# Up products of a gated FFN: three products of 256 columns, or one of 512 and one of 256 with the halves added by VectorE

## The chip, the cores and the metric

The kernel runs on one core of a Trainium2 chip (trn2). Times are device microseconds (us) of one execution. A core has TensorE (PE in the rows: MATMUL, with the weight loads under PEld), VectorE (DVE), ScalarE (ACT), GpSimd (POOL) and SyncE (SP), each with a stream of its own; they meet only at semaphores. TensorE writes its results to PSUM, eight banks of 512 f32 columns in each of 128 partitions.

## What is computed

A model of four layers over 256 tokens of width 1024. The first two layers end in this FFN; their mixers, and the two mixture-of-experts layers behind them, are not touched by the change.

```
DFF = 2816                                  # D_FF
def conv_glu_ffn(n, w_up, conv_w, conv_b, w_down):      # n: (1, 256, 1024)
    s = n.shape[1]
    gate, up = jnp.split(n @ w_up, 2, axis=-1)          # w_up: (1024, 2 * 2816)
    gp = jnp.pad(gate, ((0, 0), (CONV_WIDTH - 1, 0), (0, 0)))
    conv = conv_b
    for j in range(CONV_WIDTH):                         # 3 taps along the tokens
        conv = conv + gp[:, j:j + s] * conv_w[j]
    return (jax.nn.silu(conv) * up) @ w_down
```

## The kernel before

**Numbers.** Every large product is made of fp32r operands that are split in two: `w_high` is the weight rounded to fp32r, `w_low` the rest, and the same for x and the hidden values. `product` (L1327 to L1331) adds high by high, high by low and low by high into one PSUM region, three MATMULs with a weight load ahead of each. ScalarE writes `w_high` from the loaded `raw` chunk (L460, two halves of 1024 columns), VectorE writes `w_low` as raw minus w_high (L788, two halves). In the FFN the weights are the stationary operand and x the moving one, so the products come out turned: 128 hidden channels by 256 tokens.

**Chunks and the ring.** The weights come as chunks of 128 x 2048 f32 (1 MB) into a ring of three slots. A chunk's `raw` slot is loaded again when `w_low` of it is written, and its `w_high` and `w_low` slots are written again when TensorE has counted `chunk_used` for it. ScalarE and VectorE split a chunk two ahead (`AHEAD`) of the one in use.

**One FFN** (`glu`, once in each engine's stream) is 22 tiles of 128 channels, in 11 pairs. TensorE's order is: up, up (tiles 0 and 1); ten times a turn of up, up, down (`turn`); one last down. An up (`up`, L1511) takes one chunk: eight k steps for the gate half and eight for the up half, each step one `product`. Gate goes to columns 0 to 255 of bank 4 + u, up to columns 256 to 511 of the same bank, u being the tile's place in its pair. A down (`down`) takes one chunk and adds a pair's share to banks 0 to 3: eight products of 512 columns. The down of a turn belongs to the pair before, so a pair's hidden values have one more turn to be ready in; only the last down has no turn in between: its pair's ups stand in the last turn, with just that turn's down between them and it.

**A tile's elementwise work** (buffers `conv` and `gate` are halves of rope_a, `hid` a half of rope_b, under which names they stand in the rows):

```
ACT  wait chunk_used -> conv = Identity(bank, scale w2, bias b)   L553, then split of a chunk (u = 0)
DVE  conv[1:] += bank * w1 (L940); conv[2:] += bank * w0 (L943)
ACT  gate = Silu(conv)                                            L558
DVE  hid = gate * up half of the bank                             L946
ACT  gh = high part of hid                                        L564
DVE  gl = hid - gh                                                L948
```

**What sets the order.** It is written out by hand in each stream and does not change at run time. VectorE's turn is: split of chunk c+2, split of c+3, tile 0, tile 1, split of c+4, where c is the first chunk of the turn. ScalarE's is: split of c+2, Identity of tile 0, split of c+3, the rest of tile 0, tile 1, split of c+4. An up of tile f waits until `hid` of tile f-2 is written, because that frees its bank. Inside the loop of the program two turns stand (j = 0 and 1).

**Two reductions elsewhere** are spoken of later, both in the routing behind the FFNs and in SBUF: L1006 sums over a view `p t (g e) -> p t e g` with e = 8, in which each of the 64 elements read lies 32 bytes or more from the one before it; L1015 takes a maximum over 32 elements that lie in adjacent pairs.

Of the kernel before, what the change touches and what calls it, by code (L numbers as in the profile page):

```python
# [19 lines left out]
F32R = mybir.dt.float32r  # L20
# [135 lines left out]
def build(nc, x, stream, router, small, const, fgain, out):  # L156
    es = ExitStack()
    with es:
# [14 lines left out]
        xh = sb("x_high", [P, KT, S], F32R)  # L173
        xl = sb("x_low", [P, KT, S], F32R)
# [31 lines left out]
        hid = rope_b[:, :, 0:S]  # L206
# [79 lines left out]
        hss_ready, hrs_ready, lam_sum, lam_exp = map(sem, ("head_ssq_ready", "head_rstd_ready", "lam_sum", "lam_exp"))  # L286
        conv_init, conv_ready, silu_ready, hid_ready, g_high, g_low = map(sem, (
# [152 lines left out]
        def _(act):  # L440
# [101 lines left out]
            def glu(l):  # L542
# [3 lines left out]
                def tile(f, fi, u, c, off, lookahead):  # L546

                    act.wait_ge(chunk_used, off * RING + (c + 1))
                    if not isinstance(f, int) or f >= 2 or l:
                        act.wait_ge(hid_ready, fi - 1)  # L550
                    wcol = sml[:, bass.ds(f + (nc_w + 2 * FT), 1)]
                    bcol = sml[:, bass.ds(f + nc_b, 1)]
                    nc.scalar.activation(conv[:, u, :], B[4 + u][:, 0:S], ACT.Identity, bias=bcol,  # L553
                                         scale=wcol).then_inc(conv_init, 1)
                    if lookahead is not None:
                        split(lookahead, off)
                    act.wait_ge(conv_ready, fi * 2 + 2)
                    nc.scalar.activation(gate[:, u, :], conv[:, u, :], ACT.Silu).then_inc(silu_ready, 1)  # L558
# [9 lines left out]
                tile(0, f0, 0, c0, 0, c0 + 1 + AHEAD)  # L568
                high_part(f0, 0, 0, c0)
                tile(1, f0 + 1, 1, c0 + 1, 0, None)  # L570
                high_part(f0 + 1, 1, 0, c0)
                with act.Fori(0, (NFB - 1) // 2) as i:
                    for j in range(2):
                        c = c0 + 2 + 3 * j
                        for u in range(2):
                            fi = i * 4 + (f0 + 2 + 2 * j + u)
                            f = i * 4 + (2 + 2 * j + u)
                            if u == 0:
                                split(c + AHEAD, i * 2)
                            tile(f, fi, u, c + u, i * 2, c + 1 + AHEAD if u == 0 else None)  # L580
                            high_part(fi, u, (1 + j) % 2, i * 6 + (c - 3))
                        split(c + 2 + AHEAD, i * 2)
# [187 lines left out]
        def _(dve):  # L770
# [161 lines left out]
            def glu(l):  # L932
                c0 = C_FFN[l]
                cw = SMALL["conv_w"][0] + l * 3 * FT

                def tile(f, fi, u, buf):
# [3 lines left out]
                    stt(conv[:, u, 1:S], B[4 + u][:, 0:S - 1], w1, conv[:, u, 1:S], ALU.mult, ALU.add)\  # L940
                        .then_inc(conv_ready, 1)
                    dve.wait_ge(conv_ready, fi * 2 + 1)
                    stt(conv[:, u, 2:S], B[4 + u][:, 0:S - 2], w0, conv[:, u, 2:S], ALU.mult, ALU.add)\  # L943
                        .then_inc(conv_ready, 1)
                    dve.wait_ge(silu_ready, fi + 1)
                    tt(hid[:, u, :], gate[:, u, :], B[4 + u][:, S:2 * S], ALU.mult).then_inc(hid_ready, 1)  # L946
# [4 lines left out]
                plain(c0, 1)  # L951
                split(c0 + 1 + AHEAD)
                tile(0, f0, 0, 0)
                tile(1, f0 + 1, 1, 0)
                with dve.Fori(0, (NFB - 1) // 2) as i:
                    for j in range(2):
                        c = c0 + 2 + 3 * j
                        split(c + AHEAD, i * 2)
                        split(c + 1 + AHEAD, i * 2)
                        for u in range(2):  # L960
                            tile(i * 4 + (2 + 2 * j + u), i * 4 + (f0 + 2 + 2 * j + u), u, (1 + j) % 2)
# [362 lines left out]
        def _(pe):  # L1324
# [182 lines left out]
            def glu(l):  # L1507
# [3 lines left out]
                def up(fi, u, c, off, q=None):  # L1511

                    if u is not None and (not isinstance(off, int) or c >= c0 + 2):
                        pe.wait_ge(hid_ready, fi - 1)
                    s = c % RING
                    for g in range(2):
                        for k in range(KT):
# [3 lines left out]
                            if q is not None and g == 0:  # L1521

                                pe.wait_ge(t_low, T_BASE[q] + max(k, 2) + 1)
                            ins = product(B[4 + u][:, g * S:(g + 1) * S], wh[:, s, lo:lo + P], wl[:, s, lo:lo + P],
                                          xh[:, k, :], xl[:, k, :], k == 0, k == KT - 1)
# [544 lines left out]
```

## Time and profile before

| | |
|---|---|
| runs | 1417.95, 1418.06, 1421.6 us; median 1418.06 |
| profiled execution | span 1422.4 us from the first to the last instruction, 19426 instructions; no other time of its own is given |
| busy in it | PE 1306.8 us (92%), PEld 944.6, DVE 674.7 (47%), ACT 550.1 (39%) |
| the two FFNs | about 156 to 347 us and 487 to 677 us of the span |
| mean granted TensorE clock | 0.967 of full speed |

A row of the timeline begins with the start and the duration in us, then the engine, the line of the kernel, the operation, output<-inputs by the program's names, shapes and count; in brackets stands the engine's idle time before it and what ended that. A MATMUL's own duration contains its run through the array and overlaps the next one, so TensorE's pace is read from start to start. A merged row (x2, x4) gives the first start and the whole stretch.

### The profile page before, as it was taken

Reading aid. Unit: us, or ns where it says so; the run is one execution under the profiler, and the core shown is the slowest. Engines: PE = TensorE matmul, PEld = TensorE weight load, DVE = VectorE, ACT = ScalarE, POOL = GpSimd, SP = SyncE. Lnnn points to the kernel's source line nnn. Section 1 sums busy time; section 2 is a strip of 40 time slices with the busy share of each in tenths; the row PEclk is TensorE's granted clock in tenths of the full one; section 3 lists DMA queues with packets and bytes.
Section 4 is the critical chain, followed back from the end, with each engine's and each line's share of the span. In section 5 each row is a group of like instructions: output and inputs, shape, how many; then the busy total and the mean of one; then the engine's idle time right before and its main releaser. Section 6 shows DMA issues by size and latency. Waiting matters only on the chain.

```text
span 1422.4 us, 19426 instructions
## 1 busy us (share of the span) xinstructions
PE 1306.8 (92%) x7252; PEld 944.6 (66%) x7252; DVE 674.7 (47%) x1399; ACT 550.1 (39%) x1072; POOL 32.4 (2%) x68
## 2 busy tenths in 40 slices
PE   7999999999998899999889799998869987999986
PEld 5877899997877799999677533443257874444322
DVE  6656566666758666666657510110056463111102
ACT  5354554445445545554475211110045541111101
POOL 0000000000001000000100000000000000000000
PEclk9999999999999999999899899999979798999999
DMA  8531455554550365555413899999953087999996
GB/s 338 178 118 60 128 194 183 189 187 155 178 178 1 117 210 177 177 181 188 165 62 120 324 364 411 410 411 411 409 204 133 1 323 282 410 411 410 411 410 254
DMA packets 92188, 336.83 MB, mean 237 GB/s; under 512 B 10512, under 2 KB 10640, under 8 KB 91984
## 3 DMA queue, kind: packets, MB, share of 16 engines
q1 hardware_dynamic: 92016, 335.51, 64.2%
q8 instruction: 49, 0.80, 0.2%
q0 software_dynamic: 96, 0.30, 0.1%
q14 instruction: 27, 0.22, 0.0%
HBM read 334.72 MB, written 1.05 MB: 236 GB/s over the span
## 4 chain that ended last, share of the span: by engine, by line
PE 75%; DMA 9%; DVE 7%; ACT 4%; issue 2%; SPq 1%; POOL 1%; DVEq 0%; ACTq 0%; POOLq 0%
PE bank L1329 15%; PE bank L1331 14%; PE bank L1330 14%; PE bank L1602 11%; DMA expert_part<-stream 8%; PE bank L1631 6%; PE bank L1448 2%; PE bank L1557 2%; DVE w_low L788 2%; PE bank L1456 1%; SPq L373 1%; ACT tok L470 1%; PE bank L1644 1%; PE bank L1392 1%; PE bank L1405 1%
## 5 line engine op out<-in xcount | busy, mean ns | idle before, releaser
L788 DVE TENSOR_TENSOR w_low<-raw,w_high 128x1024 fp32r<-128x1024 f32 (+1 forms) x246 | 285.6, 1212 | 134.9 <-ACT w_high L460 134.7
L460 ACT ACTIVATE w_high<-raw 128x1024 fp32r<-128x1024 f32 (+1 forms) x246 | 241.9, 1042 | 52.9 <-PE bank L1331 47.1
L1602 PE MATMUL bank<-expert_part,slots_x 128*64 128x512 f32 x1024 | 232.2, 595 | 19.4 <-DMA expert_part<-stream 17.7
L1329 PE MATMUL bank<-x_high,w_high 128*128 128x256 f32 (+1 forms) x712 | 203.1, 285 | 2.9 <-DVE x_low L807 2.7
L1331 PE MATMUL bank<-x_high,w_low 128*128 128x256 f32 (+1 forms) x712 | 202.5, 284 | 0.0
L1330 PE MATMUL bank<-x_low,w_high 128*128 128x256 f32 (+1 forms) x712 | 202.5, 284 | 0.0
L1602 PEld LDWEIGHTS bank<-expert_part,slots_x 128*64 128x64 f32 x1024 | 74.3, 137 | 171.8 <-issue 170.2
L1329 PE MATMUL bank<-w_high,x_high 128*128 128x512 f32 (+1 forms) x416 | 164.6, 396 | 4.2 <-DVE x_low L807 2.3
L1097 DVE SCALAR_TENSOR_TENSOR expert_hid<-expert_gate,combine,bank 128x256 f32<-128x256 f32 x32 | 15.4, 480 | 314.9 <-ACT expert_gate L613 314.9
L1330 PE MATMUL bank<-w_low,x_high 128*128 128x512 f32 (+1 forms) x416 | 162.4, 390 | 0.0
L1331 PE MATMUL bank<-w_high,x_low 128*128 128x512 f32 (+1 forms) x416 | 162.1, 390 | 0.0
L1329 PEld LDWEIGHTS bank<-x_high,w_high 128*128 128x128 f32 (+1 forms) x712 | 136.6, 192 | 5.4 <-issue 3.7
L1330 PEld LDWEIGHTS bank<-x_low,w_high 128*128 128x128 f32 (+1 forms) x712 | 136.7, 192 | 1.2
L1331 PEld LDWEIGHTS bank<-x_high,w_low 128*128 128x128 f32 (+1 forms) x712 | 136.6, 192 | 0.4
L613 ACT ACTIVATE expert_gate<-bank 128x256 f32<-128x256 f32 x32 | 12.3, 384 | 283.7 <-PE bank L1602 283.7
L1631 PE MATMUL bank<-expert_part,hid_turned 128*64 128x512 f32 x512 | 117.4, 599 | 4.0 <-ACT hid_turned L617 3.8
L1329 PEld LDWEIGHTS bank<-w_high,x_high 128*128 128x128 f32 x416 | 79.3, 191 | 22.2 <-DVE w_low L788 3.7
L1331 PEld LDWEIGHTS bank<-w_high,x_low 128*128 128x128 f32 x416 | 79.2, 190 | 15.4
L1330 PEld LDWEIGHTS bank<-w_low,x_high 128*128 128x128 f32 x416 | 79.3, 191 | 14.5
L1631 PEld LDWEIGHTS bank<-expert_part,hid_turned 128*64 128x64 f32 x512 | 34.0, 136 | 64.3 <-issue 55.4
L1331 PE MATMUL bank<-w_high,hid_low 128*128 128x512 f32 x176 | 69.5, 395 | 0.0
L1330 PE MATMUL bank<-w_low,hid_high 128*128 128x512 f32 x176 | 69.4, 394 | 0.0
(247 smaller groups left out, 1612.3 us busy)
## 6 DMA issues: line engine op xcount, KB each, us to landing
expert_part<-stream SPq DMA_DIRECT2D x384, 512.0 KB, 15.2
raw<-stream SPq DMA_DIRECT2D x244, 512.0 KB, 5.1
const_sb<-const SPq DMA_DIRECT2D x1, 2070.0 KB, 13.4
residual<-x SPq DMA_DIRECT2D x2, 512.0 KB, 4.2
final_gain<-fgain SPq DMA_DIRECT2D x2, 512.0 KB, 9.1
out<-residual SPq DMA_DIRECT2D x2, 512.0 KB, 2.6
small_sb<-small SPq DMA_DIRECT2D x1, 765.0 KB, 5.9
rope_a<-router POOLq DMA_DIRECT2D x2, 144.0 KB, 2.8
```

The lines of the kernel that those rows point to most:

```text
L373: sync.dma_start(slot[at][half][:, :], stream[c][:, lo:lo + CH // 2]).then_inc(slot_in[at][half], 16)
L460: nc.scalar.activation(wh[:, u, cols], raw[:, u, cols], ACT.Copy).then_inc(w_high, 1)
L470: nc.scalar.activation(tok[:, t, cols], h[:, t, cols], ACT.Square, scale=float(D) ** -0.5, accum_out=ssq[:, t, half:half + 1]).then_inc(ss ...
L788: tt(wl[:, u, cols], raw[:, u, cols], wh[:, u, cols].bitcast(F32), ALU.subtract).then_inc(w_low, 1)
L1097: stt(m_hidden[:, :], m_gate[:, :], comb[:, p:p + 1], B[0][:, DE:2 * DE], ALU.mult, ALU.mult).then_inc(m_hid, 1)
L1329: mm(o, ah, bh, start=start, stop=False, **kw)
L1330: mm(o, ah, bl, start=False, stop=False, **kw)
L1331: return mm(o, al, bh, start=False, stop=stop, **kw)
L1448: ins = mm(o[:, lo:hi], q[:, t * P:(t + 1) * P], k[:, 0:hi - lo], start=True, stop=True)
L1557: ins = mm(o[:, kk * 4 * CAP:(kk + 1) * 4 * CAP], src[:, t, k * P:(k + 1) * P], pick[:, g % 2, t, :], start=kk == 0 and t == 0 and src is ...
L1602: ins = mm(B[0][half * CAP:(half + 1) * CAP, :], xg[p // 4 % 2][:, k, x_of], w[half][:, kk * 512:(kk + 1) * 512], start=k == 0, stop=k == ...
L1631: ins = mm(B[2 + col][rows, :], hidT[:, k, rows], w[half][:, col * 512:(col + 1) * 512], start=p % 2 == 0 and k == 0, stop=p % 2 == 1 and ...
```

## The change

The two parts of x become one buffer, so that one moving operand of 512 columns holds x_high and x_low of a k step. A high weight tile is loaded once and meets both: the product goes to all 512 columns of a bank, high by high left, high by low right. The low weight tile then meets x_high alone and adds to the left half. So a k step has two MATMULs and two weight loads in place of three and three; the columns streamed stay 768. Gate and up now take a bank each, and a tile two (4 + 2u and 5 + 2u, four in all as TensorE has banks 4 to 7 here). VectorE adds the two halves of each bank with a reduction over a view in which the halves are the innermost axis, into `gate_sum` (other half of rope_b) and `up_sum` (qk_tok, idle here); Identity, the taps and the product with up read those from SBUF. An up now waits for `up_sum` of the tile two before it.

```diff
-        xh = sb("x_high", [P, KT, S], F32R)
-        xl = sb("x_low", [P, KT, S], F32R)
+        x_both = sb("x_high_low", [P, 2, KT, S], F32R)
+        xh, xl = x_both[:, 0, :, :], x_both[:, 1, :, :]
...
-        hid = rope_b[:, :, 0:S]
+        hid, gate_sum = rope_b[:, :, 0:S], rope_b[:, :, S:2 * S]
+        up_sum = qk_tok[:, :, 0:S]
...
# ScalarE, tile
-                    act.wait_ge(chunk_used, off * RING + (c + 1))
+                    act.wait_ge(gate_sum_ready, fi + 1)
...
-                    nc.scalar.activation(conv[:, u, :], B[4 + u][:, 0:S], ACT.Identity, bias=bcol,
+                    nc.scalar.activation(conv[:, u, :], gate_sum[:, u, :], ACT.Identity, bias=bcol,
...
# VectorE
+                def sums(u, c, off):
+                    g, b = B[4 + 2 * u], B[5 + 2 * u]
+                    dve.wait_ge(chunk_used, off * RING + (c + 1))
+                    for bank, total, ready in ((g, gate_sum, gate_sum_ready), (b, up_sum, up_sum_ready)):
+                        halves = bank[:, :].rearrange("p (x s) -> p s x", x=2)
+                        nc.vector.tensor_reduce(total[:, u, :], halves, AX.X, ALU.add).then_inc(ready, 1)
...
-                    stt(conv[:, u, 1:S], B[4 + u][:, 0:S - 1], w1, conv[:, u, 1:S], ALU.mult, ALU.add)\
+                    stt(conv[:, u, 1:S], gate_sum[:, u, 0:S - 1], w1, conv[:, u, 1:S], ALU.mult, ALU.add)\
...
                     dve.wait_ge(silu_ready, fi + 1)
-                    tt(hid[:, u, :], gate[:, u, :], B[4 + u][:, S:2 * S], ALU.mult).then_inc(hid_ready, 1)
+                    dve.wait_ge(up_sum_ready, fi + 1)
+                    tt(hid[:, u, :], gate[:, u, :], up_sum[:, u, :], ALU.mult).then_inc(hid_ready, 1)
...
                         split(c + AHEAD, i * 2)
+                        sums(0, c, i * 2)
                         split(c + 1 + AHEAD, i * 2)
                         for u in range(2):
+                            if u:
+                                sums(1, c + 1, i * 2)
                             tile(i * 4 + (2 + 2 * j + u), i * 4 + (f0 + 2 + 2 * j + u), u, (1 + j) % 2)
                         split(c + 2 + AHEAD, i * 2)
...
# TensorE, up
-                        pe.wait_ge(hid_ready, fi - 1)
+                        pe.wait_ge(up_sum_ready, fi - 1)
...
-                            ins = product(B[4 + u][:, g * S:(g + 1) * S], wh[:, s, lo:lo + P], wl[:, s, lo:lo + P],
-                                          xh[:, k, :], xl[:, k, :], k == 0, k == KT - 1)
+                            o = B[4 + 2 * u + g]
+                            mm(o[:, :], wh[:, s, lo:lo + P], x_both[:, :, k, :], start=k == 0, stop=k == KT - 1,
+                               skip_group_check=True)
+                            ins = mm(o[:, 0:S], wl[:, s, lo:lo + P], xh[:, k, :], start=False, stop=k == KT - 1,
+                                     skip_group_check=True)
```

How the instructions stand, in three places. The rows come from the two built programs and hold no time; ISA and REGISTER_ALU rows work out loop-dependent counts and addresses.

VectorE in the first turn that stands in the loop, from the second half of the split of chunk c+2 to the first tile. Before:

```order
L788 TENSOR_TENSOR w_low<-raw,w_high 128x1024 [waits w_high_ready]
L787 REGISTER_ALU
L788 TENSOR_TENSOR w_low<-raw,w_high 128x1024 [waits w_high_ready]
L787 REGISTER_ALU
L788 TENSOR_TENSOR w_low<-raw,w_high 128x1024 [waits w_high_ready]
L939 ISA
L940 ISA [waits conv_init]
L940 SCALAR_TENSOR_TENSOR rope_a<-bank,small_sb,rope_a 128x255
L942 ISA
L943 ISA [waits conv_ready]
L943 SCALAR_TENSOR_TENSOR rope_a<-bank,small_sb,rope_a 128x254
```

and in the changed program:

```order
L790 TENSOR_TENSOR w_low<-raw,w_high 128x1024 [waits w_high_ready]
L940 ISA
L943 TENSOR_REDUCE rope_b<-bank 128x256 [waits chunk_used]
L943 TENSOR_REDUCE qk_tok<-bank 128x256
L789 REGISTER_ALU
L790 TENSOR_TENSOR w_low<-raw,w_high 128x1024 [waits w_high_ready]
L789 REGISTER_ALU
L790 TENSOR_TENSOR w_low<-raw,w_high 128x1024 [waits w_high_ready]
L948 ISA
L949 ISA [waits conv_init]
L949 SCALAR_TENSOR_TENSOR rope_a<-rope_b,small_sb,rope_a 128x255
```

Two reductions, the first of them waiting for TensorE, now stand between the split of c+2 and that of c+3; two more stand between tile 0 and tile 1.

ScalarE in the same turn, from the high part of tile 0 to Silu of tile 1. Before:

```order
L564 ACTIVATE hid_high<-rope_b 128x256 [waits chunk_used]
L548 REGISTER_ALU
L553 ISA [waits hid_ready,chunk_used]
L553 ACTIVATE rope_a<-bank,small_sb 128x256
L557 ISA
L558 ACTIVATE rope_a<-rope_a 128x256 [waits conv_ready]
```

and in the changed program:

```order
L566 ACTIVATE hid_high<-rope_b 128x256 [waits chunk_used]
L550 REGISTER_ALU
L555 ISA [waits hid_ready,gate_sum_ready]
L555 ACTIVATE rope_a<-rope_b,small_sb 128x256
L559 ISA
L560 ACTIVATE rope_a<-rope_a 128x256 [waits conv_ready]
```

Identity waited for TensorE's chunk and now waits for VectorE's reduction of the gate bank.

TensorE at the first k steps of the first up, with bank numbers. Before:

```order
L1329 MATMUL bank4<-x_high,w_high 128x256
L1330 MATMUL bank4<-x_low,w_high 128x256
L1331 MATMUL bank4<-x_high,w_low 128x256
L1329 MATMUL bank4<-x_high,w_high 128x256
L1330 MATMUL bank4<-x_low,w_high 128x256
L1331 MATMUL bank4<-x_high,w_low 128x256
```

and in the changed program:

```order
L1540 MATMUL bank4<-x_high_low,w_high 128x512
L1542 MATMUL bank4<-x_high_low,w_low 128x256
L1540 MATMUL bank4<-x_high_low,w_high 128x512
L1542 MATMUL bank4<-x_high_low,w_low 128x256
L1540 MATMUL bank4<-x_high_low,w_high 128x512
```

Three MATMULs of 256 columns have become one of 512 and one of 256, in the same place.

## Rows read from the trace of the kernel before

**Rows 1.** The page, part 1: busy time, share of the span, instructions.

```profile
PE 1306.8 (92%) x7252; PEld 944.6 (66%) x7252; DVE 674.7 (47%) x1399; ACT 550.1 (39%) x1072; POOL 32.4 (2%) x68
```

**Rows 2.** Windows in both FFNs: us, busy PE, PEld, DVE, ACT, POOL, clock, DMA, GB/s.

```profile
175.00:345.00 170.00, 170.00 (x1179) 158.76 (x1178) 106.78 (x142) 84.37 (x121) 0.00 (x0) 1.00 0.56 183
505.00:675.00 170.00, 170.00 (x1182) 158.89 (x1181) 106.67 (x142) 85.15 (x122) 0.00 (x0) 1.00 0.56 182
```

**Rows 3.** TensorE's waits from 160 to 350 us: total, times, longest.

```profile
PE bank L1381 <- DVE tok L797: 2.2, 1, 2.2
```

**Rows 4.** Timeline of TensorE in one turn: its first, its down's first, the next turn's first.

```profile
255.66 0.28 PE L1329 MATMUL bank<-x_high,w_high 128*128 128x256 f32 x1
255.78 0.28 PE L1330 MATMUL bank<-x_low,w_high 128*128 128x256 f32 x1
...
267.17 0.39 PE L1329 MATMUL bank<-w_high,hid_high 128*128 128x512 f32 x1
...
272.74 0.28 PE L1329 MATMUL bank<-x_high,w_high 128*128 128x256 f32 x1
```

**Rows 5.** Timeline of TensorE, 512 columns in a projection at full clock.

```profile
706.72 0.39 PE L1329 MATMUL bank<-w_high,x_high 128*128 128x512 f32 x1
706.95 0.39 PE L1330 MATMUL bank<-w_low,x_high 128*128 128x512 f32 x1
```

**Rows 6.** Timeline of TensorE, 256 columns at half clock.

```profile
159.82 0.41 PE L1329 MATMUL bank<-x_high,w_high 128*128 128x256 f32 x1
160.04 0.41 PE L1330 MATMUL bank<-x_low,w_high 128*128 128x256 f32 x1
```

**Rows 7.** Timeline of VectorE over one turn.

```profile
246.29 2.36 DVE L788 TENSOR_TENSOR w_low<-raw,w_high 128x1024 fp32r<-128x1024 f32 x2 [3.68 <-ACT w_high L460]
248.57 0.48 DVE L940 SCALAR_TENSOR_TENSOR rope_a<-bank,small_sb,rope_a 128x255 f32<-128x255 f32 x1
...
251.15 0.42 DVE L948 TENSOR_TENSOR hid_low<-rope_b,hid_high 128x256 fp32r<-128x256 f32 x1 [0.57 <-ACT hid_high L564]
251.72 0.48 DVE L940 SCALAR_TENSOR_TENSOR rope_a<-bank,small_sb,rope_a 128x255 f32<-128x255 f32 x1
...
254.21 0.42 DVE L948 TENSOR_TENSOR hid_low<-rope_b,hid_high 128x256 fp32r<-128x256 f32 x1 [0.48 <-ACT hid_high L564]
255.16 4.63 DVE L788 TENSOR_TENSOR w_low<-raw,w_high 128x1024 fp32r<-128x1024 f32 x4 [0.52 <-ACT w_high L460]
263.29 2.36 DVE L788 TENSOR_TENSOR w_low<-raw,w_high 128x1024 fp32r<-128x1024 f32 x2 [3.50 <-ACT w_high L460]
```

**Rows 8.** Timeline of ScalarE, Identity of tile 0 and the split behind it.

```profile
261.75 0.56 ACT L553 ACTIVATE rope_a<-bank,small_sb 128x256 f32<-128x256 f32 x1 [3.78 <-PE bank L1331]
262.21 2.00 ACT L460 ACTIVATE w_high<-raw 128x1024 fp32r<-128x1024 f32 x2
```

**Rows 9.** Groups of VectorE instructions by form: count, busy us, mean ns, idle before.

```profile
L835 DVE TENSOR_SCALAR qk_tok<-bank 128x512 f32<-128x512 f32 x4 | 2.6, 685 | 3.0 <-PE bank L1331 3.0
...
L1006 DVE TENSOR_REDUCE qk_tok<-qk_tok 128x16 f32<-128x64 f32 x2 | 0.5, 264 | 0.1
...
L1015 DVE TENSOR_REDUCE qk_tok<-qk_tok 128x8 f32<-128x32 f32 x2 | 0.4, 186 | 0.1
```

**Rows 10.** Timeline of ScalarE, Identity of the first tile of the first FFN.

```profile
164.34 0.57 ACT L553 ACTIVATE rope_a<-bank,small_sb 128x256 f32<-128x256 f32 x1 [2.47 <-PE bank L1331]
```

**Rows 11.** Timeline of TensorE, the last product of the first FFN.

```profile
346.43 0.40 PE L1331 MATMUL bank<-w_high,hid_low 128*128 128x512 f32 x1
```

**Rows 12.** Windows behind the second FFN, where TensorE pauses.

```profile
677.50:679.20 1.70, 0.04 (x1) 0.00 (x0) 0.94 (x3) 1.61 (x6) 0.86 (x2) 1.00 0.87 316
679.20:684.00 4.80, 0.00 (x0) 0.00 (x0) 3.03 (x3) 2.67 (x8) 3.90 (x5) 0.53 0.40 147
684.00:689.00 5.00, 4.79 (x19) 4.43 (x20) 2.62 (x7) 2.05 (x6) 0.86 (x2) 0.50 0.00 0
```

More of the change, by code:

```diff
@@ L286, in build @@
         hss_ready, hrs_ready, lam_sum, lam_exp = map(sem, ("head_ssq_ready", "head_rstd_ready", "lam_sum", "lam_exp"))
+        gate_sum_ready, up_sum_ready = sem("gate_sum_ready"), sem("up_sum_ready")
         conv_init, conv_ready, silu_ready, hid_ready, g_high, g_low = map(sem, (
@@ L544, in glu, with tile @@
                 nc_b, nc_w = SMALL["conv_b"][0] + l * FT, SMALL["conv_w"][0] + l * 3 * FT
-                def tile(f, fi, u, c, off, lookahead):
-                    act.wait_ge(chunk_used, off * RING + (c + 1))
+                def tile(f, fi, u, off, lookahead):
+                    act.wait_ge(gate_sum_ready, fi + 1)
                     if not isinstance(f, int) or f >= 2 or l:
@@ L567, in glu @@
                 plain(c0, 1)
-                tile(0, f0, 0, c0, 0, c0 + 1 + AHEAD)
+                tile(0, f0, 0, 0, c0 + 1 + AHEAD)
                 high_part(f0, 0, 0, c0)
-                tile(1, f0 + 1, 1, c0 + 1, 0, None)
+                tile(1, f0 + 1, 1, 0, None)
                 high_part(f0 + 1, 1, 0, c0)
@@ L579, in glu @@
                                 split(c + AHEAD, i * 2)
-                            tile(f, fi, u, c + u, i * 2, c + 1 + AHEAD if u == 0 else None)
+                            tile(f, fi, u, i * 2, c + 1 + AHEAD if u == 0 else None)
                             high_part(fi, u, (1 + j) % 2, i * 6 + (c - 3))
@@ L939, in tile @@
                     dve.wait_ge(conv_init, fi + 1)
-                    stt(conv[:, u, 1:S], B[4 + u][:, 0:S - 1], w1, conv[:, u, 1:S], ALU.mult, ALU.add)\
+                    stt(conv[:, u, 1:S], gate_sum[:, u, 0:S - 1], w1, conv[:, u, 1:S], ALU.mult, ALU.add)\
                         .then_inc(conv_ready, 1)
                     dve.wait_ge(conv_ready, fi * 2 + 1)
-                    stt(conv[:, u, 2:S], B[4 + u][:, 0:S - 2], w0, conv[:, u, 2:S], ALU.mult, ALU.add)\
+                    stt(conv[:, u, 2:S], gate_sum[:, u, 0:S - 2], w0, conv[:, u, 2:S], ALU.mult, ALU.add)\
                         .then_inc(conv_ready, 1)
                     dve.wait_ge(silu_ready, fi + 1)
-                    tt(hid[:, u, :], gate[:, u, :], B[4 + u][:, S:2 * S], ALU.mult).then_inc(hid_ready, 1)
+                    dve.wait_ge(up_sum_ready, fi + 1)
+                    tt(hid[:, u, :], gate[:, u, :], up_sum[:, u, :], ALU.mult).then_inc(hid_ready, 1)
                     dve.wait_ge(g_high, fi + 1)
@@ L951, in glu @@
                 plain(c0, 1)
+                sums(0, c0, 0)
                 split(c0 + 1 + AHEAD)
                 tile(0, f0, 0, 0)
+                sums(1, c0 + 1, 0)
                 tile(1, f0 + 1, 1, 0)
```

## The prediction

> **What bounds the kernel now.** I read the page's busy times first: TensorE 92%, VectorE 47% [rows 1]. The change touches the two FFNs alone, so the windows inside them come next: in 170 us TensorE has no idle time at the full clock, VectorE is busy for 63% and ScalarE for 50% [rows 2]. TensorE's waits say the same: from 160 to 350 us it waits once, at the norm behind the FFN, and never for a weight split or a hidden value [rows 3]. Today the FFN runs at TensorE's pace.
>
> TensorE's turn is read from start to start [rows 4]. The 96 products of two ups take 267.17 - 255.66 = 11.51 us, 0.120 us each; the 24 of a down 272.74 - 267.17 = 5.57, 0.232 each. A turn is 17.08 us.
>
> VectorE's share of busy time would make it look free for some more work. Its timeline says otherwise [rows 7]. In one turn it has one real gap, 3.5 us ahead of the w_low of chunk c+3, where it waits for TensorE to finish chunk c. Everything else is a chain that goes back and forth with ScalarE, and all the gaps of about half a microsecond in it are ScalarE's share of the chain, not slack. The question is whether four reductions a turn fit in that gap.
>
> **The change, part by part.**
>
> *TensorE, up.* 22 x 2 x 16 = 704 k steps lose one of three MATMULs and one weight load. Columns stay 768. A step costs 3 x 0.120 = 0.360 us; after, one 512-column product and one of 256. In a projection 512 columns take 0.23 [rows 5], in the down 0.232 [rows 4]: 0.350 together. That saves 0.010 a step, 0.32 a turn, 7 us in all if TensorE stays the bound: the array is paid by the column, and only the fixed part of a MATMUL goes. The turn would be 5.57 + 32 x 0.350 = 16.77 us. A buffer's wait is loosened too (an up waits for `up_sum`, which comes ahead of `hid`); it ends no wait today, so it brings nothing.
>
> *VectorE, four reductions a turn.* Call one R. It reads 512 elements of PSUM and writes 256. The nearest contiguous row, 512 elements from PSUM, takes 685 ns [rows 9]; that is the lower end, since R has as much to read. But the view steps between the halves at each element: 1024 bytes ahead, then back to the next column. Two reductions bear on that [rows 9]. The one over adjacent pairs takes 186 ns for 32 elements; from 512 elements at 685, 480 more elements cost 499 ns, 1.04 ns each, so it pays the contiguous price. At that price 64 elements would be 219 ns; the row with 32-byte steps takes 264, so 45 more, 0.70 ns for each element. 512 x 0.70 = 360 on top of 685: R = 1.04 us. I take this value: it is the same operation, and like R it never reads two neighbours in a row. The upper end, a second full cycle for every element, is 685 + 512 x 1.04 = 1.22 us.
>
> The Trainium skill (Advanced Engine Details and Errata, PSUM Cachelines) has a rule against this view: PSUM lines are 8 bytes, and every two consecutive elements should be contiguous; it names matmuls as what is slowed. By that rule R would lie at 1.04 or above. That rule in PSUM is shown by no row here; the strided row reads SBUF.
>
> *The chain of a turn.* I walk it from the start of the first reduction of a turn to the same point of the next, with distances from the rows. A hand-over between engines is taken as 0.04, small against the rest.
> 1. Gate reduction of tile 0: R. The up reduction runs behind it while ScalarE works.
> 2. ScalarE: 0.04, from Identity to the split behind it 262.21 - 261.75 = 0.46 [rows 8], and from there to VectorE's w_low 263.29 - 262.21 = 1.08 [rows 7, 8]: 1.58. Before, TensorE released Identity; now VectorE does, and behind Identity is queued the w_high that VectorE needs next.
> 3. Two w_low: 248.57 - 246.29 = 2.28 [rows 7].
> 4. Tile 0, from L940 to L940 of tile 1: 251.72 - 248.57 = 3.15 [rows 7].
> 5. Gate and up reductions of tile 1: consecutive VectorE instructions overlap by about 0.07 (four w_low of 1.21 in 4.63), so 2R - 0.14. Identity (0.56) hides under the second of them.
> 6. Tile 1 and the hand-over to w_high: 255.16 - 251.72 = 3.44 [rows 7].
> 7. Four w_low, start to next start: 4 x 1.14 = 4.56 [rows 7].
>
> The sum is 14.87 + 3R (only the up reduction of tile 0 is hidden): 16.9 for R = 0.69, 18.0 for 1.04, 18.5 for 1.22. All are above TensorE's 16.77. So VectorE and ScalarE's chain sets the pace from here, and the MATMULs saved are worth nothing. Spare w_low time (5 us: the second up's chunk is ready at 256.3, used at 261.4) puts off TensorE's first stall by some turns, but does not save them: the last down needs the last pair's hidden values, and these stand at the end of the chain.
>
> *One FFN.* The first up ends at 164.3 [rows 10]. The first pair goes through the same chain with two w_low fewer: 14.87 + 3R - 2.28 = 12.6 + 3R to the first reduction of turn 1. Nine more turns, 9 x (14.87 + 3R). Then to the end of `gl` of the last pair: steps 1 to 5 and 254.21 + 0.42 - 251.72 = 2.91, 9.8 + 3R. In sum 164.3 + 12.6 + 133.8 + 9.8 + 33R = 320.5 + 33R. Today the last down starts at 346.43 - 23 x 0.232 = 341.1 [rows 11]. The difference is 33R - 20.6: 2.2 us for R = 0.69, 13.7 for 1.04, 19.7 for 1.22. Two FFNs: 4, 27 and 39 us.
>
> *The clock.* TensorE is ahead of the chain at the end: it has done the last turn's down and then waits about 5 us for the hidden values. Behind the second FFN 1.7 us without products were enough that the granted clock fell from 1.00 to 0.50, and it stayed there through 5 us of work afterwards [rows 12]. At half clock 256 columns take 0.22 [rows 6], so 512 take twice that. Four to five microseconds of the last down's 5.6 at half clock cost about 2 us; 0 and 4.6 (all of it) are the ends. I take 2 for each FFN, 4 in all. The pauses of about 1.2 us in each turn I cost at nothing, since each is followed by 16 us of products.
>
> *Everything else.* Identity, the taps and hid read SBUF instead of PSUM: taken as equal. Loads follow w_low as before, at a DMA share of 0.56 [rows 2], so they have room.
>
> Sum: 27 + 4 = 31 us. The profiled span is 1422.4, 4.3 above the median 1418.06 (0.3%); the differences above are within that one execution, and I add them to the median: 1418 + 31 = 1449, rounded up to 1450.
>
> **The rivals.**
> - *The stepped read costs nothing* (R = 0.69). For it: two alternating lines are fewer than the four of the strided row, and no row shows PSUM read this way. Then 4 us from the chain and 0 to 4 from the clock: 1422 to 1427.
> - *Every element costs two cycles* (R = 1.22): 39 + 4, 1461. For it: the halves are 1024 bytes apart, further than the row's 32. The rule of the Trainium skill above leans the same way.
> - *Faster.* The reduction is paid by its 256 outputs, 0.42 us as a 256-element instruction (L948) [rows 7]. The chain is then 16.1, under 16.77; TensorE sets the pace and the 0.32 a turn comes through: 1418 - 7 = 1411. It decides below R = 0.63. Against it: the reduction rows grow with what they read [rows 9].
> - *No change:* R near 0.69 and hand-overs 0.1 us a turn shorter than I take them, so that what is lost at the last down is won in the turns: 1418 within 4.
> - *TensorE streams the joint operand slower*, because its two pieces lie 8 KB apart. At 0.30 instead of 0.23 a turn is 19.0 us; 22 pairs of ups lose 1.9 each: 1460. Nothing in the rows is for it.
>
> **How the numbers follow.** Chances: forecast 0.41, two cycles 0.22, stepped read free 0.22, slow stream 0.04, faster 0.05, no change 0.06. A measurement of this kernel tells 0.3% (4.3 us) from no change. Slower takes the first four, 0.89. The forecast alone gives 1440 to 1456. The range reaches from the free read to two cycles with a colder clock: 1423 to 1466.
>
> **What would show it.** R in the group of the reductions: 1.0 us is right, 0.69 or 1.22 are the rivals. VectorE's turn near 18.0 us from one first reduction to the next, with no wait for TensorE left. TensorE: 0.35 per k step, about 1.2 us of waiting in each turn for w_low, and about 5 us ahead of the last down for hid_low, the clock falling there. If VectorE still waits for TensorE at the first reduction, the chain is mis-summed and the time will be lower than forecast.

## The result, and the profile after

| | median | ratio to the kernel before, 95% interval |
|---|---|---|
| changed kernel, first measurement | 1441.43 us (1418.46 for the kernel before beside it) | 1.0171 [1.0134, 1.0209] |
| the same file, second measurement | 1440.79 us | 1.0134 [1.0105, 1.0163] |
| the kernel before again, as a control | 1421.32 us | 1.0002 [0.9977, 1.0026] |

It is slower by 1.3% to 1.7%. The forecast was 1450, the range 1423 to 1466. The profiled run of the first measurement took 1460.8 us, some 20 us more than the other four (1440.3 to 1444.9), because in the mixer of the first layer the granted clock was 0.58 from 85 to 145 us; so wherever a stretch is compared in length, the trace is that of the second measurement (span 1437.2 us). A stretch is called cold below where the granted clock stands at the lower of its two levels, 1.2 GHz (0.50 in the rows) and not 2.4.

Page of the first measurement, part 1, against [rows 1]: 704 products and loads fewer, VectorE 55 us busier.

```profile
PE 1333.7 (91%) x6548; PEld 930.6 (64%) x6548; DVE 729.8 (50%) x1487; ACT 554.1 (38%) x1072; POOL 31.5 (2%) x68
```

Windows in both FFNs, against [rows 2] (same columns). TensorE no longer fills the 170 us, and VectorE went from 107 to 128:

```profile
175.00:345.00 170.00, 165.88 (x860) 139.66 (x859) 127.81 (x181) 86.65 (x124) 0.00 (x0) 0.99 0.54 177
525.00:695.00 170.00, 166.82 (x867) 140.89 (x866) 127.11 (x178) 84.80 (x119) 0.00 (x0) 0.99 0.55 179
```

The groups of 175 to 345 us by line (count, busy us, mean ns, idle before): the reductions, and Identity, which took 0.56 us from PSUM in [rows 8].

```profile
L943 DVE TENSOR_REDUCE rope_b<-bank 128x256 f32<-128x512 f32 x20 | 13.7, 685 | 0.1
L943 DVE TENSOR_REDUCE qk_tok<-bank 128x256 f32<-128x512 f32 x19 | 13.0, 682 | 0.0
L555 ACT ACTIVATE rope_a<-rope_b,small_sb 128x256 f32<-128x256 f32 x19 | 11.4, 602 | 37.1 <-DVE rope_b L943 37.1
```

R is 0.685 us, the price of a contiguous read [rows 9], and not 1.04.

TensorE's waits in the second trace, 160 to 350 us (total, times, longest), where [rows 3] have one row for the norm and none for a split or a hidden value:

```profile
PE bank L1344 <- DVE hid_low L958: 4.1, 1, 4.1
PE bank L1540 <- DVE w_low L790: 3.0, 6, 2.0
```

The waits for `w_low` come to 3.0 us in six places, where the prediction expected about 1.2 us in each turn.

VectorE's timeline over one turn of the second trace, first reduction to first reduction, against [rows 7]. There is no wait for TensorE in it, and a turn is 278.85 - 261.59 = 17.26 us (nine turns from 175.02 to 330.79: 17.31 each):

```profile
261.59 0.68 DVE L943 TENSOR_REDUCE rope_b<-bank 128x256 f32<-128x512 f32 x1
262.19 0.68 DVE L943 TENSOR_REDUCE qk_tok<-bank 128x256 f32<-128x512 f32 x1
264.04 2.36 DVE L790 TENSOR_TENSOR w_low<-raw,w_high 128x1024 fp32r<-128x1024 f32 x2 [1.17 <-ACT w_high L462]
266.31 0.48 DVE L949 SCALAR_TENSOR_TENSOR rope_a<-rope_b,small_sb,rope_a 128x255 f32<-128x255 f32 x1
...
269.24 0.68 DVE L943 TENSOR_REDUCE rope_b<-bank 128x256 f32<-128x512 f32 x1
269.84 0.68 DVE L943 TENSOR_REDUCE qk_tok<-bank 128x256 f32<-128x512 f32 x1
270.84 0.48 DVE L949 SCALAR_TENSOR_TENSOR rope_a<-rope_b,small_sb,rope_a 128x255 f32<-128x255 f32 x1 [0.33 <-ACT rope_a L555]
...
274.30 4.63 DVE L790 TENSOR_TENSOR w_low<-raw,w_high 128x1024 fp32r<-128x1024 f32 x4 [0.52 <-ACT w_high L462]
278.85 0.68 DVE L943 TENSOR_REDUCE rope_b<-bank 128x256 f32<-128x512 f32 x1
```

**The end of an FFN.** The prediction took the start of the last down as the end. The timeline of VectorE there, of the kernel before:

```profile
339.55 0.42 DVE L948 TENSOR_TENSOR hid_low<-rope_b,hid_high 128x256 fp32r<-128x256 f32 x1 [0.48 <-ACT hid_high L564]
340.50 4.63 DVE L788 TENSOR_TENSOR w_low<-raw,w_high 128x1024 fp32r<-128x1024 f32 x4 [0.52 <-ACT w_high L460]
345.05 2.51 DVE L921 TENSOR_TENSOR residual<-residual,bank 128x512 f32<-128x512 f32 x4
348.17 0.75 DVE L797 TENSOR_SCALAR tok<-residual,rstd 128x1024 f32<-128x1024 f32 x1 [0.62 <-POOL rstd L405]
```

and of the changed kernel, second trace:

```profile
342.53 0.43 DVE L958 TENSOR_TENSOR hid_low<-rope_b,hid_high 128x256 fp32r<-128x256 f32 x1 [0.48 <-ACT hid_high L566]
343.48 4.63 DVE L790 TENSOR_TENSOR w_low<-raw,w_high 128x1024 fp32r<-128x1024 f32 x4 [0.52 <-ACT w_high L462]
348.03 1.87 DVE L923 TENSOR_TENSOR residual<-residual,bank 128x512 f32<-128x512 f32 x3
350.32 0.69 DVE L923 TENSOR_TENSOR residual<-residual,bank 128x512 f32<-128x512 f32 x1 [0.42 <-PE bank L1346]
351.15 0.75 DVE L799 TENSOR_SCALAR tok<-residual,rstd 128x1024 f32<-128x1024 f32 x1
```

From the end of the last `hid_low` to the norm it is 348.17 - 339.97 = 8.20 us before and 351.15 - 342.96 = 8.19 after: four w_low of the next weights (4.6), four additions of the last down's banks (2.5) and the norm. TensorE's last down runs beside them in both kernels. In the kernel before no addition waits for it, so VectorE's queue behind the last hidden value sets the end of an FFN there already, and what counts is when that value is there. In the changed kernel the last addition does wait, 0.42 us, for a last down that ran cold in part; here that costs nothing, because it takes the place of the norm's own wait for GpSimd's rstd (0.62 before). In the second FFN such waits add 0.5 us (12.64 and 13.18 in the table). The stretches between norms and these marks, from the timelines (us; the first number of a pair is the first FFN's). The "first gate product read" is the start of the first Identity in the kernel before and of the first reduction in the changed one:

| trace | norm to first gate product read | from there to the last `hid_low` | on to the next norm | FFN |
|---|---|---|---|---|
| before | 13.2, 11.3 | 175.6, 175.7 | 8.20, 12.64 | 197.0, 199.6 |
| before, control | 11.3, 11.3 | 175.6, 175.7 | 8.21, 12.66 | 195.1, 199.6 |
| changed, second | 12.3, 13.1 | 182.2, 182.3 | 8.19, 13.18 | 202.8, 208.6 |

### The profile page after: what moved, and what is told of

Same layout as the page of the kernel before. It is cut to its first block, busy times and chain, and to the rows that moved or that the text cites. A ratio compares the mean times of both kernels' runs of the same rounds, so it can differ in the third digit from the quotient of the medians.

```text
span 1458.9 us, 18190 instructions
## 1 busy us (share of the span) xinstructions
PE 1333.7 (91%) x6548; PEld 930.6 (64%) x6548; DVE 729.8 (50%) x1487; ACT 554.1 (38%) x1072; POOL 31.5 (2%) x68
## 4 chain that ended last, share of the span: by engine, by line
PE 54%; DVE 15%; ACT 9%; DMA 9%; issue 9%; POOL 1%; DVEq 1%; ACTq 1%; SPq 0%; POOLq 0%
PE bank L1620 11%; DMA expert_part<-stream 9%; PE bank L1344 7%; PE bank L1346 7%; PE bank L1345 7%; PE bank L1649 6%; DVE w_low L790 5%; ACT w_high L462 3%; PE bank L1463 3%; PE bank L1575 2%; DVE rope_b L943 2%; PE bank L1471 2%; DVE rope_a L952 1%; DVE rope_a L949 1%; DVE rope_b L956 1%
## 5 line engine op out<-in xcount | busy, mean ns | idle before, releaser
L1540 PE MATMUL bank<-x_high_low,w_high 128*128 128x512 f32 x704 | 252.2, 401 | 9.4 <-DVE w_low L790 5.9
L1542 PE MATMUL bank<-x_high_low,w_low 128*128 128x256 f32 x704 | 198.3, 282 | 0.0
L1344 PE MATMUL bank<-w_high,x_high_low 128*128 128x512 f32 (+1 forms) x416 | 164.3, 395 | 3.3 <-DVE x_high_low L809 1.4
L1540 PEld LDWEIGHTS bank<-x_high_low,w_high 128*128 128x128 f32 x704 | 133.5, 190 | 45.3 <-DVE w_low L790 7.4
L1345 PE MATMUL bank<-w_low,x_high_low 128*128 128x512 f32 (+1 forms) x416 | 161.7, 389 | 0.0
L1346 PE MATMUL bank<-w_high,x_high_low 128*128 128x512 f32 (+1 forms) x416 | 161.6, 388 | 0.0
L1542 PEld LDWEIGHTS bank<-x_high_low,w_low 128*128 128x128 f32 x704 | 134.2, 191 | 0.8
L615 ACT ACTIVATE expert_gate<-bank 128x256 f32<-128x256 f32 x32 | 12.3, 385 | 283.9 <-PE bank L1620 283.9
L1344 PEld LDWEIGHTS bank<-w_high,x_high_low 128*128 128x128 f32 x416 | 79.1, 190 | 21.1 <-DVE w_low L790 2.6
L1346 PEld LDWEIGHTS bank<-w_high,x_high_low 128*128 128x128 f32 x416 | 78.8, 190 | 15.4
L1345 PEld LDWEIGHTS bank<-w_low,x_high_low 128*128 128x128 f32 x416 | 79.0, 190 | 14.4
L1344 PE MATMUL bank<-w_high,hid_high 128*128 128x512 f32 x176 | 71.0, 403 | 8.0 <-DVE hid_low L958 8.0
L508 ACT ACTIVATE probs<-scores_masked,neg_max 128x128 f32<-128x128 f32 x96 | 42.8, 446 | 80.0 <-DVE neg_max L848 79.9
```

The lines of the kernel that those rows point to most:

```text
L508: ins = nc.scalar.activation(pr[:, a % 2, lo:hi], sm[:, a % 2, lo:hi], ACT.Exp, bias=nmax[:, a, t:t + 1], scale=-1.0, accum_out=den[:, a, ...
L1344: mm(o, ah, bh, start=start, stop=False, **kw)
L1345: mm(o, ah, bl, start=False, stop=False, **kw)
L1346: return mm(o, al, bh, start=False, stop=stop, **kw)
L1540: mm(o[:, :], wh[:, s, lo:lo + P], x_both[:, :, k, :], start=k == 0, stop=k == KT - 1, skip_group_check=True)
L1542: ins = mm(o[:, 0:S], wl[:, s, lo:lo + P], xh[:, k, :], start=False, stop=k == KT - 1, skip_group_check=True)
```

## Experiments

Each kernel was timed beside the kernel before on the same chip. The control, the second measurement and the two halves of the change shared one chip, the next four kernels another; the last two stood each by itself.

**r_before and r_after: both files again.**

> The kernel before, unchanged, as a control and for a second profile. Ratio 1.00. The profile tells how much of a stage's length varies from execution to execution: the first FFN, from its norm (VectorE's tok write) to the norm behind it, took 197.0 us, the second with the final norm 199.6, the stage of the first mixer 144.

> The changed kernel, unchanged. Ratio about 1.016 as first measured. In the first profile the FFNs are 6.0 and 7.7 us longer, some 14 of the 23 us between the medians. Theory A (the chain of VectorE and ScalarE with what follows from it) expects the FFNs again 6 to 8 us longer each and the rest of the program the same. Theory B (the clock) expects a further 5 to 10 us in stages outside the FFNs, with a granted clock of 0.5 there where the kernel before has 1.0.

Measured: above. The spans differ by 1437.2 - 1419.9 = 17.3 us, cut at the norms: first FFN +7.7, second +9.0, mixer of the third layer +4.7, MoE behind it -2.7, the rest -1.4. The second FFN's 9.0 are 6.6 up to the last `hid_low`, 1.9 at its start, where the clock stood at 0.57 from 489 to 497 us, and 0.5 behind it.

**pe_part_alone: the new products without the reductions.** `sums` and its waits are gone, and Identity, taps and `hid` read the left half of the banks:

```diff
-                    nc.scalar.activation(conv[:, u, :], gate_sum[:, u, :], ACT.Identity, bias=bcol,
+                    nc.scalar.activation(conv[:, u, :], B[4 + 2 * u][:, 0:S], ACT.Identity, bias=bcol,
...
-                    tt(hid[:, u, :], gate[:, u, :], up_sum[:, u, :], ALU.mult).then_inc(hid_ready, 1)
+                    tt(hid[:, u, :], gate[:, u, :], B[5 + 2 * u][:, 0:S], ALU.mult).then_inc(hid_ready, 1)
```

> TensorE's part of the change alone: one product of 512 columns and one of 256, two banks a tile, but no reductions; ScalarE and VectorE read the left half straight from PSUM, so that high by low is left out of the result. Theory A: TensorE's turn falls from 17.08 to 16.8 us, no wait inside the FFN, 7 us faster than before (ratio 0.995). Rival (the joint operand is no cheaper, or dearer): a turn of 17.1 or more, ratio 1.000 or above.

Measured: 1416.53 us, ratio 0.9969 [0.9946, 0.9993]. In its timeline two ups take 295.43 - 284.32 = 11.11 us against 11.51 in [rows 4], so a k step is 0.347 (forecast 0.350). The rows are the first product of the one and the first of the down behind it:

```profile
284.32 0.40 PE L1534 MATMUL bank<-x_high_low,w_high 128*128 128x512 f32 x1
...
295.43 0.39 PE L1338 MATMUL bank<-w_high,hid_high 128*128 128x512 f32 x1
```

From the first gate product to the last `hid_low` an FFN takes 172.7 and 172.8 us, 2.9 less than before. TensorE's term was right in kind and size, and the operand in two pieces streams like any other: the product behind it starts 0.23 to 0.24 later (0.232 in the down, [rows 4]).

**reductions_alone: the reductions with the old three products.**

```diff
-                            mm(o[:, :], wh[:, s, lo:lo + P], x_both[:, :, k, :], start=k == 0, stop=k == KT - 1,
-                               skip_group_check=True)
+                            mm(o[:, 0:S], wh[:, s, lo:lo + P], xh[:, k, :], start=k == 0, stop=False,
+                               skip_group_check=True)
+                            mm(o[:, S:2 * S], wh[:, s, lo:lo + P], xl[:, k, :], start=False, stop=k == KT - 1,
+                               skip_group_check=True)
```

> VectorE's part alone: three products of 256 columns as before, high by low going to the right half of the bank, and the four reductions a turn. Theory A: the chain sets the pace (VectorE's turn 17.3 us against TensorE's 17.1), so this is as slow as the changed kernel, ratio 1.015 to 1.018, with VectorE's turn unchanged within 0.05 us. Rival (TensorE's saving still counts under the chain): 7 us slower than the changed kernel, ratio 1.021.

Measured: 1440.57 us, ratio 1.0118 [1.0087, 1.0149]; both FFNs 182.2 us to the last `hid_low`, as in the changed kernel. With or without the joint product the stretch is equally long: the saved MATMULs are worth nothing there, and the loss is the reductions' alone.

**no_up_reduction: the gate half is added, the up half is not.**

```diff
-                    for bank, total, ready in ((g, gate_sum, gate_sum_ready), (b, up_sum, up_sum_ready)):
+                    for bank, total, ready in ((g, gate_sum, gate_sum_ready),):
```

> The changed kernel with the gate reductions alone: hid reads the left half of the up bank, so high by low is left out of up. As forecast, the up reduction of tile 1 lay on the chain: VectorE's turn would fall by 0.6 us, 12 us in all (ratio to before about 1.005). The profile of the changed kernel says instead that the tap behind it waits for ScalarE's Identity, so that reduction is hidden: turn 17.3 as with it, ratio 1.012 to 1.014.

Measured: 1439.94 us, ratio 1.0156 [1.0116, 1.0197]; 182.2 and 182.3 us to the last `hid_low`. Its VectorE rows of tile 1: without a second reduction the taps still start 1.61 us behind the first (1.60 with it, above), only the idle time before them is longer, 0.93 instead of 0.33. A turn is 237.92 - 220.66 = 17.26.

```profile
220.66 0.68 DVE L943 TENSOR_REDUCE rope_b<-bank 128x256 f32<-128x512 f32 x1
222.27 0.49 DVE L949 SCALAR_TENSOR_TENSOR rope_a<-rope_b,small_sb,rope_a 128x255 f32<-128x255 f32 x1 [0.93 <-ACT rope_a L555]
...
237.92 0.68 DVE L943 TENSOR_REDUCE rope_b<-bank 128x256 f32<-128x512 f32 x1
```

Both up reductions of a pair run beside ScalarE and cost nothing. The chain holds 2R, where the prediction had 3R.

**gate_reduction_twice: each gate reduction preceded by one more, into an unused buffer.**

```diff
+                        if bank is g:
+                            nc.vector.tensor_reduce(qk_tok[:, u, S:2 * S], halves, AX.X, ALU.add)
                         nc.vector.tensor_reduce(total[:, u, :], halves, AX.X, ALU.add).then_inc(ready, 1)
```

> The changed kernel with each gate reduction made twice, the first into a free buffer. Theory A (the chain): 0.6 us more for each of the two in a turn, turn 18.5, 13 us more for each FFN, 26 in all, ratio about 1.032. Rival (VectorE has room, the loss is the clock's): a few us more at most, ratio below 1.02.

Measured: 1465.23 us, ratio 1.0304 [1.0260, 1.0348].

```profile
207.87 0.68 DVE L944 TENSOR_REDUCE qk_tok<-bank 128x256 f32<-128x512 f32 x1
208.47 0.68 DVE L945 TENSOR_REDUCE rope_b<-bank 128x256 f32<-128x512 f32 x1
...
226.33 0.68 DVE L944 TENSOR_REDUCE qk_tok<-bank 128x256 f32<-128x512 f32 x1
```

A turn is 18.46 us (18.50 over eight), so two more gate reductions cost 1.20, which is 0.60 each, the distance of their starts. They come through in full: from the first reduction to the last `hid_low` it is 195.4 us in both FFNs, 13.1 more than in the changed kernel, about 22 times 0.60. The gate reductions lie on the path that sets the end. (The trace has the cold stretch of the first layer, as the first trace of the changed kernel has, so only stretches inside the FFNs are read from it.)

**filled_pause: TensorE's pause ahead of the last down filled.** 18 products of 512 columns into a bank that is free by then:

```diff
+                pe.wait_ge(up_sum_ready, f0 + FT - 1)
+                for _ in range(18):
+                    mm(B[4][:, :], x_both[:, 0, 0, 0:P], x_both[:, :, 1, :], start=True, stop=True)
                 pe.wait_ge(g_low, f0 + FT)
```

> The changed kernel with 18 products of 512 columns into a free bank ahead of the last down, some 4 us, about as long as TensorE's pause there. They change nothing in the result. Theory B in part (the pause costs half clock in the last down: 1.5 and 2.4 us read in its product starts): the last down back at 5.6 us, 3 to 4 us faster than the changed kernel (ratio about 1.011); if the cold stretch of 16 us in the third layer's attention hangs on that pause too, 8 us faster (1.008). Rival (the clock costs nothing here): same as the changed kernel.

Measured: 1435.23 us, ratio 1.0107 [1.0066, 1.0149]. Windows of the changed kernel (second trace; us, PE busy, clock, DMA share, GB/s):

```profile
340.00:342.00 2.00, 0.00 (x0) 1.00 0.09 35
342.00:344.00 2.00, 0.99 (x2) 0.69 0.00 0
344.00:346.00 2.00, 2.00 (x6) 0.50 0.10 23
346.00:348.00 2.00, 2.00 (x9) 0.96 0.82 254
```

and of filled_pause:

```profile
342.00:344.00 2.00, 2.00 (x10) 1.00 0.00 0
344.00:346.00 2.00, 2.00 (x11) 1.00 0.13 43
```

The clock stayed at its upper level, and the 24 products started within 5.45 us (342.85 to 348.30) instead of 6.87 (343.01 to 349.88). But the first FFN is as long as before the edit, 202.8 us: VectorE's 8.2 us behind `hid_low` cover the slower down. In the second it is 207.6 instead of 208.6, with 0.5 of that behind the last `hid_low` and the other 0.5 at the start of the FFN. So the cold last down costs 0 and 0.5 us here, not 2 each. Where it ran longer it cost more: in the trace of no_up_reduction the first FFN's took 7.9 us and the norm came 8.97 us behind `hid_low`, not 8.19. The kernel gained more than that elsewhere: the mixer of its third layer took 108.9 us, not 113.7 (below).

**sums_first: the reductions of tile 0 moved ahead of the split of chunk c+2 in VectorE's turn.** Nothing else changes.

```diff
-                        split(c + AHEAD, i * 2)
                         sums(0, c, i * 2)
+                        split(c + AHEAD, i * 2)
```

> The changed kernel with one line moved: in VectorE's turn the reductions of tile 0 stand ahead of the split of chunk c+2, so that this split (2.3 us, its w_high long ready) fills the 1.2 us that VectorE waits for ScalarE's Identity and w_high. Theory A: the chain falls to about 16.25 us, below TensorE's 16.77, TensorE sets the pace again, and only the last down's wait (2 to 3 us for each FFN) stays: about 1418, ratio 0.997 to 1.003, with 16.8 from turn to turn. Rival (the turn is not set by that idle time): as the changed kernel, 1.013.

Measured: 1420.64 us, ratio 1.0000 [0.9975, 1.0025]. VectorE's timeline over a turn:

```profile
222.42 0.69 DVE L943 TENSOR_REDUCE rope_b<-bank 128x256 f32<-128x512 f32 x1 [0.68 <-PE bank L1542]
223.03 0.68 DVE L943 TENSOR_REDUCE qk_tok<-bank 128x256 f32<-128x512 f32 x1
223.62 4.62 DVE L790 TENSOR_TENSOR w_low<-raw,w_high 128x1024 fp32r<-128x1024 f32 x4
...
239.17 0.69 DVE L943 TENSOR_REDUCE rope_b<-bank 128x256 f32<-128x512 f32 x1 [0.68 <-PE bank L1542]
```

The turn is 16.75 us, and VectorE waits for TensorE again. The 1.17 us in which VectorE waited for `w_high` behind Identity are gone: Identity is released before the split of c+2, and ScalarE writes `w_high` of c+3 while VectorE works on c+2. Without its wait the chain would be 16.75 - 0.68 = 16.1, so TensorE's 16.75 is the bound. To the last `hid_low` it is 174.2 and 174.3 us, 8.0 less than in the changed kernel and 1.4 less than before the change. The FFNs are 194.8 and 199.3 us, still 2.9 and 2.7 more than without any reduction (191.9 and 196.6 in pe_part_alone): a wait of 2.2 us ahead of the last down stays, and the first reduction starts 12.3 us behind the norm. TensorE's waits from 160 to 372 us:

```profile
PE bank L1396 <- DVE tok L799: 3.1, 1, 3.1
PE bank L1344 <- DVE hid_low L958: 2.2, 1, 2.2
```

**sums_interleaved: on top of that, two reductions moved into VectorE's waits for ScalarE.**

```diff
                         .then_inc(conv_ready, 1)
+                    if not u:
+                        up_add(u)
                     dve.wait_ge(silu_ready, fi + 1)
...
                     tt(hid[:, u, :], gate[:, u, :], up_sum[:, u, :], ALU.mult).then_inc(hid_ready, 1)
+                    if not u:
+                        gate_add(1, c + 1, off)
                     dve.wait_ge(g_high, fi + 1)
```

> Edit on top of sums_first: the up reduction of tile 0 moves into VectorE's wait for Silu, and the gate reduction of tile 1 into its wait for the high part of hid of tile 0. In sums_first VectorE waits about 0.48 us at either place, 20 times each in 175 to 345 us, and TensorE's only stall in the FFN is 2.2 us ahead of the last down. Theory (the end of the last pair's chain is what is left to win): the two w_low chunks start 0.6 us earlier and Identity of tile 1 0.6 to 0.7 us earlier, so hid_low of the last pair comes 1.0 to 1.4 us earlier, the stall falls to 0.8 to 1.2 us, VectorE's wait for TensorE in a turn grows from 0.7 to about 1.7 us, the turn stays 16.75. An FFN is 1 to 1.4 us shorter than in sums_first, two FFNs 2 to 2.8: ratio to before 0.998. Rival (the order within the tiles does not matter, ScalarE sets the end): stall still 2.2 us, ratio 1.000.

Measured: 1420.66 us, ratio 0.9997 [0.9978, 1.0016]. TensorE's waits from 160 to 372 us:

```profile
PE bank L1547 <- DVE qk_tok L940: 1.8, 1, 1.8
PE bank L1351 <- DVE hid_low L968: 0.8, 1, 0.8
```

The stall ahead of the last down fell from 2.2 to 0.8 us as expected, but a new one of 1.8 us came up in the first turn, for the first tile's `up_sum`, which now stands behind the taps. The FFNs took 195.5 and 200.5 us, 0.7 and 1.2 longer than in sums_first, where 1.0 to 1.4 shorter was expected. The edit had put off a release that TensorE waits for there.

**sums_interleaved_2: the first tile's up reduction back in its old place.**

```diff
-                    if not u:
+                    if not u and not isinstance(f, int):
                         up_add(u)
...
                 gate_add(0, c0, 0)
+                up_add(0)
```

> The same as sums_interleaved, but the up reduction of the first tile of an FFN stands again right behind its gate reduction. In sums_interleaved TensorE's stall ahead of the last down fell from 2.2 to 0.8 us, but it waited 1.8 us (first FFN) and 0.7 us (second) for up_sum in the first turn, where that reduction had moved from 161.4 to 166.3 us. Theory (that wait took the gain): no wait for up_sum in the first turn, a stall of 0.7 to 0.8 us ahead of the last down, first FFN 193.5 to 194 us between the norms (195.5 with the wait, 194.8 in sums_first), turn 16.75; two FFNs 2.5 us shorter than in sums_interleaved; ratio to before 0.998. Rival (what is won inside the FFN is given back behind it, at the norm or by the clock): FFN stretches as in sums_first within 0.5 us and ratio 1.000.

Measured: 1424.87 us, ratio 1.0045 [1.0024, 1.0065]. Inside the FFNs the expectation came true: 193.4 and 199.1 us, the shortest of a kernel that computes everything (195.1 and 199.6 before). Yet the kernel is slower, where 0.998 was expected. In its trace the mixer of the third layer, which the edit doesn't touch, took 114.7 us instead of 109.1 in sums_interleaved. Windows from 72 to 92 us behind the norm (us, PE busy, clock, DMA share, GB/s), in sums_interleaved:

```profile
753.30:773.30 20.00, 17.05 (x117) 1.00 0.30 99
```

and in sums_interleaved_2:

```profile
772.90:792.90 20.00, 18.93 (x87) 0.52 0.09 26
```

There the clock stood at its lower level. The profiled run of sums_interleaved_2 had the cold stretch in the first layer too, so its stages stand for its timed runs only in part: these are 0.45% or 6.4 us above those of the kernel before, where the FFNs and this mixer account for 3.5 (5.7 more in the mixer, 2.2 less in the FFNs). The rest is not located.

The same stretch in the changed kernel, second trace:

```profile
767.50:787.50 20.00, 18.94 (x94) 0.57 0.09 25
```

It was cold in both traces of the changed kernel and in reductions_alone, with the mixer at 113.4 to 113.7 us. It was warm in the two of the kernel before, in filled_pause, sums_first and sums_interleaved (1.00, mixer 108.9 to 109.2), and nearly so in pe_part_alone, no_up_reduction and gate_reduction_twice (0.91, 109.3 to 109.6). So neither the reductions nor a cold last down make it cold by themselves: gate_reduction_twice has both. The instructions of this layer are the same in all, so what it does itself doesn't set them apart. It may also change from run to run of one kernel: in the second measurement one run of the changed kernel took 1428.5 us at a mean clock of 0.971, ten others 1436.8 to 1441.9 at 0.960 to 0.965, and the traced run of no_up_reduction, 1431.8 us, is the fastest of its six. One trace for each kernel can't tell that from an effect of the edit. What sets them apart was not found.

## Why the prediction was right, and where it was wrong

**Right: the sign, and the mechanism up to the end of the turns.** VectorE and ScalarE's chain took over from TensorE. reductions_alone and gate_reduction_twice show it, and TensorE's own saving came out as forecast (0.347 a k step) and was worth nothing beside it. The chain holds two reductions a turn and not three, though: with R = 0.685 the path over Identity is the longer one in step 5 by the prediction's own figures (0.685 + 0.04 + 0.56 = 1.29 against 1.23).

**Wrong: R.** "The stepped read" was sized by a row in SBUF at 1.04 us; it is 0.685. The rule of the Trainium skill (Advanced Engine Details and Errata, PSUM Cachelines), by which every two consecutive elements should be contiguous, cost this read by VectorE nothing; the page names matmuls as what is slowed. By the prediction's own formula that takes 23 of its 27 us away: the rival that the stepped read is free was true, and its 1422 to 1427 was too low.

**Wrong by the other sign: 33R - 20.6.** With R = 0.685 it gives 2.0 us for an FFN, and the first one grew by 7.7. The missing 5.7:
1. *The chain, mostly its hand-overs, 3.4.* The turn is 17.31, and the formula gives 16.93. Step 2 with R, to the w_low: 264.04 - 261.59 = 2.45, forecast 2.27. Step 5: 270.84 - 269.24 = 1.60, forecast 1.23, since it is R, a hand-over, Identity (0.60 from SBUF, not 0.56) and a hand-over back, and longer than the two reductions beside it. Step 4 was 2.93, not 3.15. The others came within 0.02. The nine turns make 3.4 and the tail 0.3, and the first pair was 0.4 quicker than its sum. The hand-over from the end of a reduction to Identity was taken as 0.04; it is 0.04 in the pair that stands ahead of the loop (reduction at 160.73, Identity at 161.45), but 0.19 inside it (251.97, 252.84), and 0.18 to 0.27 over all turns of both FFNs. Inside the loop the wait stands on an ISA row ahead of Identity, which works out the count to compare with; that this is the reason is likely, but no run takes it apart.
2. *The end, 1.2.* The comparison was made against the start of the last down, 341.1, or 176.8 behind the first Identity. VectorE's queue sets the end, and its `hid_low` was done at 339.97 in the kernel before, 175.6 behind the first Identity.
3. *The start, 1.1.* Identity of the first tile started 11.3 us behind the norm in three of the four FFNs traced of the kernel before; the first reduction starts at 12.3 at the earliest, because it stands behind four w_low on VectorE. The prediction kept 164.3 for both.

**Wrong: the clock, 2 us for each FFN.** The fall came where it was forecast, in a pause of 4.1 us instead of 5. The last down took 1.4 us longer in the first FFN for it, which cost nothing, being covered, and 0.5 us of the second. In its place the cold stretch in the mixer of the third layer, with 4.7 us, and a cold start of the second FFN, with some 0.8, came in, cases the prediction did not have.

So 1450 against 1441 is a close number by two errors of opposite sign, R too large by 23 us and all the rest too small by about 15, and not a well-sized sum.

## What to carry to other kernels

When a change adds work to an engine that is half idle, ask where in its queue the work stands and which waits it puts off: with the two reductions of tile 0 behind the split of a chunk the two FFNs grew by 16.7 us, and with these two ahead of it they were as long as before the change (0.6 us less). Take the end of a stage from the engine whose queue reaches the next stage last; here that was VectorE with the next weights and the additions, and not the products. And move a release that another engine waits for only after looking at the first turn too, where the order ahead is another.

## What was not expected of the hardware

- VectorE's sum over pairs that lie 1024 bytes apart in PSUM takes 685 ns for 512 elements, like a contiguous read of as many (685, another operation, [rows 9]).
- Identity with a scale and bias per channel takes 602 ns on 256 elements from SBUF and 556 to 562 from PSUM (means over an FFN), where the prediction took them as equal.
- VectorE to ScalarE took 0.04 us from the end of a reduction to the start of Identity ahead of the loop and 0.18 to 0.27 inside it, in every trace of a kernel with the reductions behind the split.
- A cold stretch of 17 to 20 us in a layer that no edit touches goes with 4.7 to 5.7 us, 0.3 to 0.4% of the kernel, more than the two edits that followed sums_first won inside the FFNs (1.6 us). It came and went between the traces of these kernels.
